# A two-layer transformer pair on one core: GpSimd takes two of eight residual tiles in the second block's norms, and TensorE sums all eight squared tiles

## The reference

```python
def rms_norm(x, g):
    y = xf * lax.rsqrt(jnp.mean(xf * xf, axis=-1, keepdims=True) + NORM_EPS)
    return (y * g.astype(jnp.float32)).astype(x.dtype)

def second_block(x, c, ...):
    h = x
    for layer in range(DEPTH):                       # DEPTH = 2
        mod = (cond @ ada_w[layer] + ada_b[layer])[:, None, :]
        sh1, sc1, g1, sh2, sc2, g2 = jnp.split(mod, 6, axis=-1)
        u = rms_norm(h, norm_g[layer, 0]) * (1.0 + sc1) + sh1
        y = hgrn2_mixer(u, ...) if layer % 2 == 0 else dilated_attention_mixer(u, ...)
        h = h + (1.0 + g1) * rms_norm(y, norm_g[layer, 1])
        u = rms_norm(h, norm_g[layer, 2]) * (1.0 + sc2) + sh2
        y = swiglu_ffn(u, ffn_w_in[layer], ffn_w_out[layer])
        h = h + (1.0 + g2) * rms_norm(y, norm_g[layer, 3])
    return h
```

## Time and profile before

| | us |
|---|---|
| median of three runs | 2510.79 |
| lowest, highest | 2507.38, 2510.89 |
| the profiled execution, its own time | 2507.14 |
| its span, first to last instruction | 2505.3 |
| TensorE busy (matmuls) | 2445.4, 98% of the span |
| VectorE, ScalarE, GpSimd busy | 1337.7, 568.9, 137.8 |
| mean granted TensorE clock | 0.993 of full speed |

### The profile page before, as it was taken

How to read it: one execution, slowest core, us unless ns; L and a number is a source line. 1 busy time by engine, 2 the same in 40 slices (tenths; PEclk the granted TensorE clock), 3 DMA queues, 4 the chain that set the end, 5 groups by cost and what they waited for, 6 DMA issues and landing times.

```text
span 2505.3 us, 40221 instructions
## 1 busy us (share of the span) xinstructions
PE 2445.4 (98%) x17552; PEld 1942.2 (78%) x17552; DVE 1337.7 (53%) x1899; ACT 568.9 (23%) x931; POOL 137.8 (6%) x127
## 2 busy tenths in 40 slices
PE   8999999999999999999999999999999999989998
PEld 5787898999959689873334337958999977958998
DVE  4675324788357833231221213685788677675454
ACT  1164111110213611112222222323110211222111
POOL 0002200000000022000000000000000001120000
PEclk9999999999999999999999999999999999999999
DMA  7442224796444422338999995432896344433541
GB/s 268 151 152 101 85 84 143 289 350 256 168 151 147 153 71 84 105 111 301 372 358 352 370 336 189 135 135 76 296 350 263 120 153 151 135 110 118 185 160 68
DMA packets 230510, 476.17 MB, mean 190 GB/s; under 512 B 14272, under 2 KB 44608, under 8 KB 230208
## 3 DMA queue, kind: packets, MB, share of 16 engines
q1 hardware_dynamic: 229760, 472.08, 53.4%
q10 hardware_dynamic: 576, 1.52, 0.2%
HBM read 472.50 MB, written 1.05 MB: 189 GB/s over the span
## 4 chain that ended last, share of the span: by engine, by line
PE 84%; DVE 6%; DMA 3%; ACT 3%; SPq 2%; issue 1%; POOL 1%; DVEq 0%; ACTq 0%
PE ps L1885 16%; PE ps L518 16%; PE ps L591 12%; PE ps L2428 10%; PE ps L583 9%; PE ps L2063 7%; PE ps L1262 3%; SPq L3634 2%; PE ps L898 1%; PE ps L2394 1%; DMA ring<-in_exp_w_up 1%; PE ps L2727 1%; DVE work L1545 1%; DMA work<-in_exp_w_down 1%; PE ps L1273 0%
## 5 line engine op out<-in xcount | busy, mean ns | idle before, releaser
L518 PE MATMUL ps<-xu,ring 128*128 128x256 f32 x1664 | 381.2, 382 | 9.0 <-DMA ring<-in_w_in 8.0
L518 PEld LDWEIGHTS ps<-xu,ring 128*128 128x128 f32 x1664 | 310.3, 191 | 48.9 <-issue 8.0
L591 PEld LDWEIGHTS ps<-xu,ring 128*128 128x128 f32 x2336 | 267.2, 193 | 7.4 <-issue 6.2
L591 PE MATMUL ps<-xu,ring 128*128 128x128 f32 x2336 | 269.5, 277 | 2.5 <-ACT xu L973 2.3
L1885 PE MATMUL ps<-xu,work 128*128 128x128 f32 x2112 | 238.8, 275 | 0.0
L1885 PEld LDWEIGHTS ps<-xu,work 128*128 128x128 f32 x2112 | 237.3, 192 | 0.0
L583 PE MATMUL ps<-ring,xu 128*128 128x512 f32 x520 | 229.3, 597 | 1.3 <-DVE ring L676 1.3
L583 PEld LDWEIGHTS ps<-ring,xu 128*128 128x128 f32 x520 | 98.3, 191 | 121.0 <-issue 116.8
L2428 PE MATMUL ps<-ring,work 128*32 128x512 f32 (+1 forms) x1776 | 184.9, 566 | 7.1 <-ACT ring L2499 3.7
L1885 PE MATMUL ps<-xu,ring 128*128 128x128 f32 x1584 | 181.4, 276 | 2.6 <-ACT xu L973 1.9
L1885 PEld LDWEIGHTS ps<-xu,ring 128*128 128x128 f32 x1584 | 179.0, 192 | 4.5 <-issue 3.8
(11 more groups left out here) (468 smaller groups left out, 3271.2 us busy)
## 6 DMA issues: line engine op xcount, KB each, us to landing
ring<-in_w_in SPq DMA_DIRECT2D x71, 1024.0 KB, 5.2
work<-in_ada_w SPq DMA_DIRECT2D x48, 1024.0 KB, 10.7
ring<-in_attn_w_in SPq DMA_DIRECT2D x36, 1024.0 KB, 5.2
ring<-in_ffn_w_in SPq DMA_DIRECT2D x32, 1024.0 KB, 7.6
ring<-in_exp_w_down SPq DMA_DIRECT2D x112, 256.0 KB, 5.0
ring<-in_exp_w_gate SPq DMA_DIRECT2D x88, 256.0 KB, 4.9
ring<-in_ffn_w_out SPq DMA_DIRECT2D x22, 1024.0 KB, 8.0
ring<-in_exp_w_up SPq DMA_DIRECT2D x80, 256.0 KB, 4.9
```

What stands on the lines that cost most here:

```text
L518: mm = pe.matmul(acc[:, m * T:(m + 1) * T], w[:, k, m * P:(m + 1) * P], src[:, half * 4 + k, :], start=(half == 0 and k == 0 and m % 2 == ...
L591: mm = pe.matmul(acc[:, m * P:(m + 1) * P], w[:, k, m * P:(m + 1) * P], x[:, k, :], start=(start and m == 0 and k == 0), stop=True, skip_g ...
```

## The change

GpSimd gets a function of its own, `post_pool`: at each of the four places it multiplies and adds tiles 6 and 7 in one piece of 512 columns each, and counts `h_pool`. VectorE's `post_dve` keeps tiles 0 to 3 and 4 to 5; it then waits for `h_pool` and counts `h_new` up by two with an empty instruction, so that the later waits on `h_new` still hold. VectorE's two additions of squared tiles (L2952, L2953) go. For the three norms of `DIRECT`, ScalarE squares in the order tiles 0 to 3, 6 and 7, 4 and 5 (`DIRECT_PARTS`), the middle one released by `h_pool`, and TensorE makes eight products, in the same order, where it made five. A semaphore that nobody waited for (`tab_sin`) goes too.

```diff
@@ -739,7 +740,9 @@
         BLOCKED = ("ple0", "spostf0", "spostf1")
         DIRECT = ("sffn0", "smix1", "sffn1")
         SQ_ORDER = [n for n in S_ORDER if n != "smix0"]
-        SUMMED = [n for n in SQ_ORDER if n not in BLOCKED + ("final",)]
+        SUMMED = [n for n in SQ_ORDER if n not in BLOCKED + DIRECT + ("final",)]
+        POSTS = ["spost0", "spostf0", "spost1", "spostf1"]
+        DIRECT_PARTS = ((0, 4), (6, 8), (4, 6))
         sq_blocks = area(8.5, 2048).rearrange("p (k t) -> p k t", t=T)
 
         def block_of(x, i):
@@ -790,12 +793,11 @@
             acc = take_unit(pe, f"st{name}")
             if name in DIRECT:
                 idle_products_pe(pe, acc[:, 512:768], 9)
-                for i, (a, b) in list(enumerate(PARTS))[1:]:
-                    pe.wait_ge(sq_done, 4 * n + i + 1)
+                for i, (a, b) in enumerate(DIRECT_PARTS):
+                    pe.wait_ge(sq_done, 4 * n + (1, 2, 4)[i])
                     for k in range(a, b):
-                        pe.matmul(acc[:, 0:T], mean, sqb[:, k, :], start=(k == 4), stop=False)
-                pe.wait_ge(sq_sum, SUMMED.index(name) + 1)
-                pe.matmul(acc[:, 0:T], mean, sq_acc, start=False, stop=True).then_inc(tick(psum_full), 1)
+                        mm = pe.matmul(acc[:, 0:T], mean, sqb[:, k, :], start=(k == 0), stop=(k == 5))
+                mm.then_inc(tick(psum_full), 1)
                 return
             if name == "final":
                 for i, (a, b) in enumerate(PARTS):
@@ -954,7 +956,14 @@
         def norm_act(act, name, shift=None):
             if name in ("mix0", "ffn0", "ple0", "ple1"):
                 ready_root_act(act)
-            for i, (a, b) in enumerate(PARTS):
+            for i, (a, b) in enumerate(DIRECT_PARTS if name in DIRECT else ()):
+                if i == 1:
+                    act.wait_ge(h_pool, DIRECT.index(name) + 1)
+                else:
+                    h_wait(act, name, i // 2)
+                act.activation(flat8(squares(name))[:, a * T:b * T], flat8(h)[:, a * T:b * T],
+                               ACT.Square).then_inc(tick(sq_done, 1 + i // 2), 1 + i // 2)
+            for i, (a, b) in enumerate(() if name in DIRECT else PARTS):
                 h_wait(act, name, i)
                 if name in BLOCKED:
                     sq_block_act(act, name, i, h)
@@ -2932,26 +2941,31 @@
             free(units[1])
             root_of_act(act, name)
 
-        def post_dve(dve, name, following):
+        def post_dve(dve, name):
 
             if name not in BLOCKED:
                 for i in range(3):
                     sq_dve(dve, name, i)
             yg = yg_ffn if name in BLOCKED else yg_mix
             root_dve(dve, name)
-            base = 4 * ["spost0", "spostf0", "spost1", "spostf1"].index(name)
-            for i, (a, b) in enumerate(PARTS):
+            base = 4 * POSTS.index(name)
+            for i, (a, b) in enumerate(PARTS[0:2]):
                 c = slice(a * T, b * T)
                 dve.wait_ge(y_out, base + i + 1)
                 i_ = dve.tensor_tensor(yg[:, a:b, :], yg[:, a:b, :], rbs.unsqueeze(1).broadcast_to([P, b - a, T]), ALU.mult)
                 dstep(dve, i_)
                 dve.tensor_tensor(flat8(h)[:, c], flat8(h)[:, c], flat8(yg)[:, c], ALU.add).then_inc(tick(h_new), 1)
-            if following is not None:
-                n, sqb = SQ_ORDER.index(following), flat8(squares(following))
-                dve.wait_ge(sq_done, 4 * n + 1)
-                dstep(dve, dve.tensor_tensor(half_sum, sqb[:, 0:2 * T], sqb[:, 2 * T:4 * T], ALU.add))
-                dve.tensor_tensor(sq_acc, half_sum[:, 0:T], half_sum[:, T:2 * T], ALU.add).then_inc(tick(sq_sum), 1)
-
+            dve.wait_ge(h_pool, POSTS.index(name) + 1)
+            dve.wait_ge(h_new, ticks[id(h_new)])
+            dve.nop().then_inc(tick(h_new, 2), 2)
+
+        def post_pool(pool, name):
+
+            yg = yg_ffn if name in BLOCKED else yg_mix
+            pool.wait_ge(rms_done, RMS_ORDER.index(name) + 1)
+            pool.wait_ge(y_out, 4 * POSTS.index(name) + 4)
+            pstep(pool, pool.tensor_tensor(yg[:, 6:8, :], yg[:, 6:8, :], rbs.unsqueeze(1).broadcast_to([P, 2, T]), ALU.mult))
+            pool.tensor_tensor(flat8(h)[:, 6 * T:], flat8(h)[:, 6 * T:], flat8(yg)[:, 6 * T:], ALU.add).then_inc(tick(h_pool), 1)
 
         NC = T // HG_C
         hq = area(0, 2048).rearrange("p (k t) -> p k t", t=T)
...
@@ -3575,9 +3589,9 @@
                     yield lambda: None
                     if l % 2 == 0:
                         yield lambda: (stat_pool(pool, "smix0"), heads_pool(pool, 4, 0, 8), heads_pool(pool, 5, 8, 12),
-                                       heads_pool(pool, 6, 12, 16))
+                                       heads_pool(pool, 6, 12, 16), post_pool(pool, "spost0"), post_pool(pool, "spostf0"))
                     else:
-                        yield lambda: attn_pool(pool)
+                        yield lambda: (attn_pool(pool), post_pool(pool, "spost1"), post_pool(pool, "spostf1"))
 
             def attn_pool(pool):
                 pool.wait_ge(rope_tab, 1)
```

More of the change, by code:

```diff
@@ L294, in build @@
         at_w, at_mix = sem("at_w"), sem("at_mix")
-        ple_out, plg_out, hg_v, hg_gt, tab_sin = (sem(n) for n in ("ple_out", "plg_out", "hg_v", "hg_gt", "tab_sin"))
+        ple_out, plg_out, hg_v, hg_gt = (sem(n) for n in ("ple_out", "plg_out", "hg_v", "hg_gt"))
+        h_pool = sem("h_pool")
         up_phase, snap_out, quad_out, w_sum, t_sum = (
@@ L3228, in hgrn_dve @@
                 sums_dve(dve, "sffn0", 0, 0, part)
-            post_dve(dve, "spost0", "sffn0")
+            post_dve(dve, "spost0")
         PAIRS = GH // 2
@@ L3338, in attn_act @@
             act.wait_ge(at_part, 1)
-            act.activation(sin2, sin2, ACT.Sin).then_inc(tick(tab_sin), 1)
+            act.activation(sin2, sin2, ACT.Sin)
             act.activation(cos2, cos2, ACT.Sin).then_inc(tick(rope_tab), 1)
@@ L3499, in attn_dve @@
                 sums_dve(dve, "sffn1", 0, 0, part)
-            post_dve(dve, "spost1", "sffn1")
+            post_dve(dve, "spost1")
         def stages_pe():
@@ L3557, in stages @@
                     yield lambda: (ffn_dve(dve, f"sffn{l}", gmix2, mod[:, 24:32]),
-                                   post_dve(dve, f"spostf{l}", None if l else "smix1"))
+                                   post_dve(dve, f"spostf{l}"))
             dve.nop().then_inc(tick(hid_out), 1)
```

## The result

Over all runs the changed kernel took 2514.53 us in the median (2511.55 to 2519.42, 8 runs) where the kernel before took 2509.44 (2506.17 to 2511.28, 8 runs). The ratio is 1.0024, with a 95% interval of 1.0015 to 1.0033: slower by about 6 us, with 3.8 to 8.3 as its bounds; the two medians lie 5.1 apart. The profiled execution took 2514.44 us, with a span of 2512.6.

A forecast was written before the change was run, and what follows sets the result against it. TensorE, busy 98% of the span, was taken as the bound, each norm's delay counting fully. 3 x 0.90 + 0.7 = 3.4 us gave 2510.5 over the profiled time or 2514.2 over the median; 2513.0 was named, range 2507.5 to 2517.5.

The forecast's parts named there:

- What bounds these places: At the three norms: delays count fully; TensorE's sixteen instructions, 3.56 us, follow the first square and become the bound.
- VectorE first, GpSimd next: After `rbs`: VectorE multiplies first, waiting GpSimd gets in before VectorE's first addition, making it 0.77 us late; chance 0.68.
- GpSimd first: Rival after `rbs`: GpSimd issues before VectorE, each norm 2.02 us later, 6.8 in all, 2513.9 to 2517.6; chance 0.12.
- GpSimd last: Rival: GpSimd gets in only after VectorE's four instructions, 1.6 us more a norm, 5.6 in all; chance 0.08.
- the first rival: At the four places: the engines don't hold each other up, 0.7 us less, 2506.4 to 2510.1; chance 0.12.
- The size of GpSimd's multiplication: GpSimd's 512-column multiplication by `rbs` at the four places: 1.10 us, or 1.27 as a full-operand instruction.
- the forecast's own staircase: At each norm: VectorE and GpSimd instructions alternate, TensorE ends at 7.95 instead of 7.05 us, 0.90 later.
- The end: At `spostf1`: last stores issued later, 0.7 us lost; times count from VectorE's first multiplication by `rbs` as zero.
- The sum: Whole program: three norms at 0.90 us plus 0.7 at the end, 3.4 us slower.
- the three cases: Whole-time outcomes against the kernel before: faster 0.03, within 0.2% (5 us) 0.65, slower 0.32.
- The two levels: Earlier executions taken to fall on two levels, profiled 2507.14 and median 2510.79 us; 2513.0 named between their sums.

The follow-up runs named there:

- the eight products alone: Changed kernel with GpSimd's part undone, VectorE scaling and adding all eight tiles, TensorE's eight products kept; 7.19 us a norm, ratio 1.0008 to the kernel before.
- the kernel with PSUM operands: Changed kernel with one input of each VectorE instruction in PSUM, finer parts, five idle products; 2505.08 us median, ratio 0.9983 to the kernel before.
- the control in SBUF: The PSUM-operand kernel with VectorE reading the inverse root and writing its products in SBUF again; 8.17 us at `sffn1` against 6.15, one run at 2519.15 us.
- GpSimd's part and the old sum: Changed kernel with VectorE again summing squares of tiles 0-3 and TensorE making five products; 8.02 us at `sffn0` and `sffn1`, one run at 2513.91 us.

## Why the prediction came out as it did

**What bounds these places**, right: each norm counts fully, TensorE's sum follows the first square without a gap, and it takes 3.56 us (1739.84 to 1743.40) as worked out. The cost of the eight products alone, forecast at 0.13, measured 0.14.

**VectorE first, GpSimd next**, right: GpSimd began 0.04 us behind VectorE (forecast within 0.1), and was let in ahead of VectorE's next instruction each time. The rivals with GpSimd first or GpSimd last have no place in the trace, and the first rival (no hold-up) is what the kernel with PSUM operands does, but not this one.

**The size of GpSimd's multiplication**, the term that was mis-sized. I took 1.10 us from L1803 and named 1.27 as the other end; without contention it measures 1.27 (the run with PSUM). With it the forecast's own staircase gives 1.07 a norm, and 1.09 was measured. An operand read over and over through an outer step of zero was no cheaper than a full one here, while L1803 reads other tiles in another pattern; what makes it shorter wasn't shown.

**The end**, forecast at 0.7 out of 0.6 to 0.9, measured 1.16: the second store leaves 5.85 after zero (5.68 forecast) and the third at about 6.25 (6.03 forecast), which is 0.86 later than before. The last two share their way, as the upper end said, landing after 2.3 in the median and not 2.1. The 0.7 took in too little of both.

**The sum** was 3.4 us; the stretches hold 4.4, and the runs say 6.0 with 3.8 as the lower bound. So the forecast of a small loss had the right sign and cause and was too small, and of the three cases the likeliest by my chances (within 0.2%) is not the likeliest by the measured ratio, 1.0024. What lies between 4.4 and 6.0 is inside the interval, and no experiment here places it. Of the 2.9 us by which the two profiled executions differ elsewhere, a part goes with TensorE's clock. In the attention of layer 1 the same 48 instructions (L875 and L898, then L877 and L900) were busy for 12.2 us where it had been 10.9, and the granted clock was 0.58 on the mean of 2244 to 2252 us, where it had been 0.79 from 2240 to 2248. But from `sffn0` to `spostf0` the full clock was granted in both, and that stretch grew too, from 212.07 to 212.48. Whether the change has a hand in either wasn't shown.

The time named, 2513.0, is 1.5 us from the measured median of 2514.53, closer than the sum deserves. It was lifted above 2507.14 + 3.4 by the choice between two levels; over the median of the eight runs before, 2509.44, the sum makes 2512.8.

**The two levels** of the runs before, which I put 3.65 us apart, are not there: the 8 runs cover 2506.17 to 2511.28 evenly. The choice between them stood on three runs.

## What to carry to other kernels

Before work is handed from VectorE to GpSimd, look at where both find their operands: with two SBUF inputs on VectorE and reads on GpSimd they take turns, and GpSimd needs 1.27 us for what VectorE does in 0.69, so the pair was slower than VectorE alone (8.14 us a norm against 7.19). With one of VectorE's inputs in PSUM the same split works, and at the last place, where the parts stayed those of the changed kernel, it took 0.9 us off what VectorE needs alone. And when work is made ready earlier, the fillers queued ahead of it have to be cut as well.

## What the runs showed of the hardware

An instruction that the other engine holds is recorded as longer, not as later. VectorE's addition of 1024 columns has 2.18 us in place of 1.22 and ends 1.09 behind the end of GpSimd's multiplication, so by estimate only 0.13 of its own work overlaps.

TensorE's granted clock fell at a norm in the two runs in which TensorE waited longest there. In the control in SBUF, at `smix1`, TensorE waited 1.36 us ahead of four instructions and 1.27 ahead of the other twelve, and the clock was then granted at 0.55 of full speed on the mean of three microseconds, so mostly at the lower of its levels (1.2 of 2.4 GHz). First TensorE's instructions there, then a table of stretches of time with the busy time of each engine (TensorE, its weight loads, VectorE, ScalarE, GpSimd), the granted clock, and the share and GB/s of the DMAs:

```profile
1962.34 1.13 PE L799 MATMUL ps<-xu,small 128*128 128x256 f32 x4 [1.36 <-ACT xu L979]
1964.74 4.54 PE L799 MATMUL ps<-xu,small 128*128 128x256 f32 x12 [1.27 <-ACT xu L979]
```

```profile
1962.30:1965.00 2.70, 1.39 (x5) 0.94 (x6) 2.63 (x4) 0.94 (x2) 0.45 (x1) 1.00 0.00 0
1965.00:1968.00 3.00, 3.00 (x9) 2.38 (x9) 0.94 (x6) 0.84 (x2) 0.00 (x0) 0.55 0.00 0
```

The twelve instructions took 4.54 us there and 2.86 at the other two norms of the same run, and the stretch was 9.86 us where those had 8.18 and 8.17. With GpSimd's part and the old sum TensorE waited 1.52 us at `smix1`, and the stretch was 9.00 instead of 8.02. At the other norms of the same two runs the waits were as long and the stretches 8.17 and 8.02, so a wait of this length doesn't always cost the clock. The Trainium skill, on the page "TensorE: Matmul & The Clock Gate", section "What's actually happening", says that the half clock is the default and activity lifts it; the trace agrees in that the fall came at a norm in which TensorE had waited 1.27 to 1.52 us at a time, and no run here shows what amount decides.
